# The mask's product moved from last to first in both attentions' score groups

## The chip, the cores and the metric

One core of one Trainium2 chip runs the whole kernel. The metric is device time in microseconds (us) of one execution; the kernel before takes 940.6 us (median of 3 runs, 940.55 to 940.61).

## The reference, cut to what matters

One layer of a streaming encoder on 512 tokens of width 1024. A parallel token mixer (forgetting attention with 8 heads of 64, and an mLSTM with 4 heads of 128) is followed by a cross-attention on 256 memory tokens and by a squared-ReLU MLP. What the change touches are the logits of the two mixers:

```python
# forgetting attention
logits = jnp.einsum('bhqd,bhkd->bhqk', qi, kf) + ci[..., :, None] - c[..., None, :]
logits = jnp.where(kpos[None, :] <= qpos[:, None], logits, -jnp.inf)
p = jax.nn.softmax(logits, axis=-1)
...
# mLSTM (chunkwise in the reference)
Dlog = bcum[..., :, None] - bcum[..., None, :] + ig[..., None, :]
Dlog = jnp.where(tri, Dlog, -jnp.inf)
...
Dw = jnp.exp(Dlog - m_t[..., None])
sqk = jnp.einsum('bhcld,bhcsd->bhcls', qc, kc) * Dw
```

The kernel computes the mLSTM as one causal attention over all 512 tokens, with the same decay and mask.

## The kernel before, in words

**Products.** Nearly all of TensorE's work is dense products of a weight with an activation, each operand split into a high and a low part of type fp32r; three products (high by high, high by low, low by high) are summed into one PSUM bank. A "half" (line 1504) is 4 slabs of 128 rows, so 12 products of 128 x 128 by 512 columns.

**Order.** `make_steps` writes out one list of steps by hand. Each engine walks through the same list and does its own part of every step; semaphores tie the engines together. The attention's steps are put before or after numbered halves, so that TensorE runs dense products while VectorE (DVE) and ScalarE (ACT) do the softmax work.

**Forgetting attention.** It has 16 tasks: 4 pairs of heads times 4 blocks of 128 queries. Block i looks at 128(i+1) keys. A task lies two halves behind the one before. `pair_scores` (from line 1587) fills bank 2 for the first head of the pair and bank 3 for the second: four products of 64 rows each (line 1602: three for the split scores and one for the decay; the two heads use rows 0 to 63 and 64 to 127), then the mask. The mask's product (line 1604) is bf16, `ident_b` by `hide_b`, 128 x 128 by 128 columns; it adds -1e30 above the diagonal of the last 128 keys. The last mask product raises `s_fscore`. DVE takes the row maximum (line 1367), ACT the exponential (990), DVE normalises (1375), TensorE transposes (1614, `pair_turn`), ACT copies to SBUF, TensorE multiplies with the values (1629, `pair_values`). On TensorE a block of steps is values of an older task, transposes of the task before, then the scores of the new task.

**mLSTM.** It has 16 tasks too (4 heads times 4 query blocks), one half apart. `scores` (from line 1634) writes the plain product of `ml_q` and `ml_k` (fp32, line 1646, two passes in the trace) to bank 5; bank 2 or 3 takes the decay (64 rows, line 1647) and then the mask (line 1648), which raises `s_score`. DVE takes the maximum (1389), then two small operations (1391, 1393), ACT the exponential (1004), DVE the product (1398), which raises `s_prob`. The scores of task t wait for `s_prob` of task t-1. After each head DVE also normalises the head's output (lines 1410 to 1428), and TensorE transposes it (1693).

**Weights.** ACT rounds each slab to `w_hi` (line 795), DVE forms `w_lo` (line 1093); these stand in the same lists as the attention's steps.

Of the kernel before, what the change touches and what calls it, by code (L numbers as in the profile page):

```python
# [13 lines left out]
P = 128  # L14
# [6 lines left out]
FOX_HEADS, FOX_HD = 8, 64  # L21
# [372 lines left out]
def trunk(nc, x, mem, norm_mix, norm_xattn, norm_mem, norm_mlp, w_in, b_fox_f, b_mlstm_i, b_mlstm_f,  # L394
# [6 lines left out]
    with ExitStack() as ctx:  # L401
        def sem(name):
            return ctx.enter_context(nc.semaphore(name))

        def sb(name, shape, dt=F32):
            return ctx.enter_context(nc.sbuf_tensor(name, shape, dt))
# [3 lines left out]
        ident_b = sb("ident_b", [P, P], BF16)  # L410
        hide_b = sb("hide_b", [P, P], BF16)
        rows = FOX_HEADS + ML_HEADS
        pick = sb("pick", [P, rows], F32R)
# [35 lines left out]
        def at(name, kb, shape, dt=F32):  # L449
            return nc.alloc_sbuf_tensor_at(name, shape, dt, offset=a0 + int(kb * KB))  # L450
# [3 lines left out]
        decay = at("decay", -53, [P, P * NT * (NT + 1) // 2], F32R)  # L454
# [55 lines left out]
        bank = [two[i // 2][:, i % 2, :] for i in range(8)]  # L510
# [39 lines left out]
        s_score, s_peak, s_exp, s_prob = sem("s_score"), sem("s_peak"), sem("s_exp"), sem("s_prob")  # L550
# [24 lines left out]
        def taken(eng, g):  # L575

            eng.wait_ge(s_taken[g % 2], g // 2 + 1)
# [9 lines left out]
        def task(t):  # L587

            h, i = t // NT, t % NT
            return h, i, P * (i + 1)  # L590
# [21 lines left out]
        def decay_at(i):  # L612
            return P * i * (i + 1) // 2
# [836 lines left out]
        def _(pe):  # L1450
# [136 lines left out]
            def pair_scores(t):  # L1587
                p, i = t // NT, t % NT
                keys, tok = P * (i + 1), slice(P * i, P * i + P)
                cols = slice(decay_at(i), decay_at(i) + keys)  # L1590
                if t == 0:
                    pe.wait_ge(s_dlow, len(DECAY_TILES) + 1)
                if i == 0:
                    taken(pe, GROUP0[UNIT["fox_k"]] + p)
                if t >= 1:
                    pe.wait_ge(s_fexp, 2 * t)
                for q in range(4):
                    for d in range(2):
                        r = slice(FOX_HD * d, FOX_HD * d + FOX_HD)
                        still = pick[r, 2 * p + d:2 * p + d + 1].to_broadcast([FOX_HD, P]) if q == 3 else (fq_hi, fq_hi, fq_lo)[q][r, p, tok]  # L1600
                        moving = decay[r, cols] if q == 3 else (fk_hi, fk_lo, fk_hi)[q][r, p, 0:keys]
                        pe.matmul(bank[2 + d][:, 0:keys], still, moving, start=(q == 0), stop=False)  # L1602
                for d in range(2):
                    ins = pe.matmul(bank[2 + d][:, P * i:keys], ident_b[:], hide_b[:], start=False, stop=True)
                ins.then_inc(s_fscore, 1)

            def pair_turn(t):
# [26 lines left out]
            def scores(t):  # L1634
                h, i, keys = task(t)
                s = bank[2 + t % 2]
                cols = slice(decay_at(i), decay_at(i) + keys)
                if t == 0:
                    pe.wait_ge(s_silu, KT)
                    pe.wait_ge(s_fpt, N_FOX)  # L1640
                    pe.wait_ge(s_fexp, 2 * N_FOX)
                else:
                    pe.wait_ge(s_prob, t)
                if t >= 2:
                    pe.wait_ge(s_exp, t - 1)
                pe.matmul(bank[5][:, 0:keys], ml_q[:, h, P * i:P * i + P], ml_k[:, h, 0:keys], start=True, stop=True)  # L1646
                pe.matmul(s[:, 0:keys], pick[0:64, FOX_HEADS + h:FOX_HEADS + h + 1].to_broadcast([64, P]), decay[0:64, cols], start=True, stop=False)  # L1647
                pe.matmul(s[:, P * i:keys], ident_b[:], hide_b[:], start=False, stop=True).then_inc(s_score, 1)

            def x_scores(t):  # L1650
                h, i = (t - X0) // NT, t % NT
# [70 lines left out]
            for step, n in steps:  # L1722
# [4 lines left out]
                elif step == "parameters":  # L1727
                    pe.wait_ge(s_param, 16 * 4)
                    pe.transpose(bank[6][:, 0:n_param], param_rows[:], ident[0:n_param, 0:n_param])\
                      .then_inc(s_pturned, 1)  # L1730
                elif step == "gates":
                    gates()
                elif step == "gate_turn":
                    pe.wait_ge(s_grows, 1)
                    for i in range(NT):
                        ins = pe.matmul(bank[7][:, 16 * i:16 * i + 16], gate_rows[:, P * i:P * i + P],
                                        pick_row[0:48, :], start=True, stop=True)
                    ins.then_inc(s_gturn, 1)
                elif step == "decay":
                    decays()  # L1740
                elif step == "pair_scores":
                    pair_scores(n)
                elif step == "pair_turn":
                    pair_turn(n)
                elif step == "pair_values":
                    pair_values(n)
                elif step == "scores":
                    x_scores(n) if n >= X0 else scores(n)
                elif step == "turn":
                    turn(n)  # L1750
                elif step == "values":
                    values(n)
                elif step == "ml_turn":
                    ml_turn(n)
                elif step == "x_values":
                    x_values(n)
# [30 lines left out]
```

## Time and profile before

| | |
|---|---|
| median of 3 runs | 940.6 us |
| the profiled execution's own time | 940.86 us |
| its span | 939.1 us |
| TensorE (PE) busy | 926.9 us, 99% |
| weight loads (PEld) busy | 757.5 us, 81% |
| VectorE busy | 552.2 us, 59% |
| ScalarE busy | 427.8 us, 46% |
| granted TensorE clock | 0.998 of full speed |

Busy times are of one profiled execution. PE is the matmul part of TensorE and PEld its weight loads, which can lie beside the matmuls. A matmul's end is modelled, so its start and the distance to the next start are better read than its duration. The forgetting attention's scores lie between 86 and 205 us, the mLSTM's between 224 and 297 us.

### The profile page before, as it was taken

How to read it: one execution, taken by the hardware profiler on the slowest of the kernel's cores; microseconds unless marked ns; L12 is line 12 of the kernel's file. 1: busy time of each engine (PE TensorE's matmuls, PEld its weight loads, DVE VectorE, ACT ScalarE, POOL GpSimd, SP SyncE). 2: the span in 40 equal slices, each digit the busy share in tenths (PEclk: the TensorE clock that was granted, in tenths of full speed). 3: DMA queues.
4: the chain of work that ended last, by engine and by line, in shares of the span. 5: the costliest groups of instructions: out<-in, count | busy, mean ns of one | idle time of the engine just before them, and what ended most of it. 6: DMA issues, size and time to landing. Idle time of an engine off the chain costs nothing.

```text
span 939.1 us, 11910 instructions
## 1 busy us (share of the span) xinstructions
PE 926.9 (99%) x4614; PEld 757.5 (81%) x4614; DVE 552.2 (59%) x997; ACT 427.8 (46%) x744; POOL 15.6 (2%) x40
## 2 busy tenths in 40 slices
PE   7999999999999999999999999999999999999997
PEld 6878777777777888889888778988888888888886
DVE  5534777423557654777234544668847966885543
ACT  5544466534424323335344543466346436634523
POOL 5000000000000000000000000000000000000000
PEclk9999999999999999999999999999999999999999
DMA  7411222022201462343521432120631261062202
GB/s 273 134 36 56 89 91 77 28 76 90 90 1 45 132 227 89 112 135 112 180 90 45 135 135 90 45 90 1 206 108 45 90 224 45 1 223 92 89 1 90
DMA packets 44687, 92.10 MB, mean 98 GB/s; under 512 B 1764, under 2 KB 1864, under 8 KB 44632
## 3 DMA queue, kind: packets, MB, share of 16 engines
q1 hardware_dynamic: 43048, 86.02, 27.0%
q0 software_dynamic: 1568, 5.32, 1.7%
q8 instruction: 37, 0.61, 0.3%
q14 instruction: 18, 0.15, 0.1%
q10 hardware_dynamic: 16, 0.00, 0.0%
HBM read 89.24 MB, written 2.10 MB: 97 GB/s over the span
## 4 chain that ended last, share of the span: by engine, by line
PE 95%; DVE 2%; ACT 2%; issue 0%; POOL 0%; ACTq 0%; DVEq 0%; POOLq 0%
PE bank L1504 70%; PE bank L1535 12%; PE bank L1659 1%; PE bank L1708 1%; PE bank L1602 1%; PE bank L1629 1%; PE bank L1614 1%; PE bank L1548 1%; PE bank L1646 1%; PE bank L1686 1%; PE bank L1673 1%; ACT w_hi L795 1%; PE bank L1647 0%; PE bank L1720 0%; DVE w_lo L1093 0%
## 5 line engine op out<-in xcount | busy, mean ns | idle before, releaser
L1504 PE MATMUL bank<-act_hi,w_hi 128*128 128x512 f32 (+1 forms) x640 | 247.7, 387 | 0.1
L1504 PE MATMUL bank<-act_hi,w_lo 128*128 128x512 f32 (+1 forms) x640 | 242.7, 379 | 0.0
L1504 PE MATMUL bank<-act_lo,w_hi 128*128 128x512 f32 (+1 forms) x640 | 242.4, 379 | 0.0
L1089 DVE TENSOR_TENSOR w_lo<-stage,w_hi 128x1024 fp32r<-128x1024 f32 x130 | 153.2, 1222 | 65.0 <-ACT w_hi L795 64.7
L795 ACT ACTIVATE w_hi<-stage 128x1024 fp32r<-128x1024 f32 x130 | 130.3, 1051 | 90.4 <-PE bank L1504 31.7
L1504 PEld LDWEIGHTS bank<-act_hi,w_lo 128*128 128x128 f32 x640 | 120.4, 188 | 23.1
L1504 PEld LDWEIGHTS bank<-act_hi,w_hi 128*128 128x128 f32 x640 | 120.6, 188 | 21.9 <-DVE w_lo L1089 0.6
L1504 PEld LDWEIGHTS bank<-act_lo,w_hi 128*128 128x128 f32 x640 | 120.6, 188 | 21.4
L1504 PE MATMUL bank<-w_hi,act_hi 128*128 128x512 f32 (+1 forms) x264 | 102.9, 390 | 3.8 <-DVE act_lo L1321 2.0
L1504 PE MATMUL bank<-w_hi,act_lo 128*128 128x512 f32 (+1 forms) x264 | 101.2, 383 | 0.0
L1504 PE MATMUL bank<-w_lo,act_hi 128*128 128x512 f32 (+1 forms) x264 | 101.1, 383 | 0.0
L1093 DVE SCALAR_TENSOR_TENSOR w_lo<-stage,gain_col,w_hi 128x512 fp32r<-128x512 f32 x88 | 60.3, 747 | 26.4 <-ACT w_hi L795 26.4
L1504 PEld LDWEIGHTS bank<-w_hi,act_hi 128*128 128x128 f32 x264 | 49.6, 188 | 14.5 <-issue 2.8
L1504 PEld LDWEIGHTS bank<-w_hi,act_lo 128*128 128x128 f32 x264 | 49.6, 188 | 9.8
L795 ACT ACTIVATE w_hi<-stage,gain_col 128x512 fp32r<-128x512 f32 x88 | 56.2, 713 | 2.5 <-PE bank L1504 2.5
L1504 PEld LDWEIGHTS bank<-w_lo,act_hi 128*128 128x128 f32 x264 | 49.7, 188 | 9.3 <-issue 0.2
L1221 DVE TENSOR_TENSOR act_lo<-ff,act_hi 128x512 fp32r<-128x512 f32 (+1 forms) x32 | 18.9, 592 | 60.2 <-ACT act_hi L795 60.0
L865 ACT ACTIVATE ff<-bank 128x512 f32<-128x512 f32 x32 | 19.0, 594 | 49.1 <-PE bank L1504 49.1
L1535 PE MATMUL bank<-w_hi,act_hi 128*128 128x512 f32 x96 | 37.3, 389 | 0.0
L1535 PE MATMUL bank<-w_lo,act_hi 128*128 128x512 f32 x96 | 37.3, 389 | 0.0
L1535 PE MATMUL bank<-w_hi,ff_lo 128*128 128x512 f32 x96 | 37.3, 389 | 0.0
L795 ACT ACTIVATE act_hi<-bank 128x512 fp32r<-128x512 f32 x32 | 17.6, 596 | 35.1 <-PE bank L1548 29.7
(290 smaller groups left out, 1290.7 us busy)
## 6 DMA issues: line engine op xcount, KB each, us to landing
stage<-in_w_in SPq DMA_DIRECT2D x20, 1024.0 KB, 4.9
stage<-in_w_mlp_in SPq DMA_DIRECT2D x16, 1024.0 KB, 5.2
stage<-in_w_mlp_out SPq DMA_DIRECT2D x16, 1024.0 KB, 5.5
stage<-in_w_xkv SPq DMA_DIRECT2D x8, 1024.0 KB, 5.0
stage<-in_w_mix_out SPq DMA_DIRECT2D x4, 1024.0 KB, 4.9
stage<-in_w_xq SPq DMA_DIRECT2D x4, 1024.0 KB, 6.0
stage<-in_w_xo SPq DMA_DIRECT2D x4, 1024.0 KB, 5.0
x_tok<-in_x SPq DMA_DIRECT2D x4, 512.0 KB, 7.0
```

What stands on the lines that cost most here:

```text
L795: return act.activation(dst, src, ACT.Copy, **k)
L865: act.activation(ff[:, t, :], b[:], ACT.Relu).then_inc(free, 1)
L1089: dve.tensor_tensor(w_lo[:, r:r + 2, :], stage_pair(pair), w_hi[:, r:r + 2, :].bitcast(F32), ALU.subtract).then_inc(s_low, 1)
L1093: ins = dve.scalar_tensor_tensor(w_lo[:, r + d, :], stage_pair(pair)[:, d, :], gain_of(pair, d), w_hi[:, r + d, :].bitcast(F32), ALU.mult, ...
L1221: dve.tensor_tensor(act2_lo[:, t, toks], ff[:, t, toks], act2_hi[:, t, toks].bitcast(F32), ALU.subtract).then_inc(s_al, 1)
L1504: ins = pe.matmul(dst, still[q], moving[q], start=(k == 0 and q == 0), stop=(k == nk - 1 and q == 2))
L1535: ins = pe.matmul(dst, s, w[:, slab % RING, :], start=(u == 0 and g == 0), stop=(u == 3 and g == 2))
L1548: ins = pe.transpose(bank[2 + 2 * (n % 2) + b][:, P * q:P * q + P], scaled[:, n % 2, P * k:P * k + P], ident[:])
L1602: pe.matmul(bank[2 + d][:, 0:keys], still, moving, start=(q == 0), stop=False)
L1614: ins = pe.transpose(bank[4 + d][:, P * j:P * j + P], (prob, prob_b)[t % 2][:, d, P * j:P * j + P], ident[:])
L1629: ins = pe.matmul(bank[6 + p % 2][r:r + FOX_HD, P * i:P * i + P], fox_v[:, j, col:col + FOX_HD], prob_t[:, d, P * j:P * j + P], start=(j = ...
L1646: pe.matmul(bank[5][:, 0:keys], ml_q[:, h, P * i:P * i + P], ml_k[:, h, 0:keys], start=True, stop=True)
```

## The change

The mask's product becomes the first into its bank and starts the sum. The scores and decays are added to it; the last decay product raises the semaphore. The number and shapes of the products are the same. In the mLSTM the mask also goes ahead of the product into bank 5.

```diff
@@ pair_scores
+                for d in range(2):
+                    pe.matmul(bank[2 + d][:, P * i:keys], ident_b[:], hide_b[:], start=True, stop=True)
                 for q in range(4):
                     for d in range(2):
...
-                        pe.matmul(bank[2 + d][:, 0:keys], still, moving, start=(q == 0), stop=False)
-                for d in range(2):
-                    ins = pe.matmul(bank[2 + d][:, P * i:keys], ident_b[:], hide_b[:], start=False, stop=True)
+                        ins = pe.matmul(bank[2 + d][:, 0:keys], still, moving, start=False, stop=(q == 3),
+                                        skip_group_check=True)
                 ins.then_inc(s_fscore, 1)
@@ scores
+                pe.matmul(s[:, P * i:keys], ident_b[:], hide_b[:], start=True, stop=True)
                 pe.matmul(bank[5][:, 0:keys], ml_q[:, h, P * i:P * i + P], ml_k[:, h, 0:keys], start=True, stop=True)
-                pe.matmul(s[:, 0:keys], pick[0:64, FOX_HEADS + h:FOX_HEADS + h + 1].to_broadcast([64, P]), decay[0:64, cols], start=True, stop=False)
-                pe.matmul(s[:, P * i:keys], ident_b[:], hide_b[:], start=False, stop=True).then_inc(s_score, 1)
+                pe.matmul(s[:, 0:keys], pick[0:64, FOX_HEADS + h:FOX_HEADS + h + 1].to_broadcast([64, P]), decay[0:64, cols],
+                          start=False, stop=True, skip_group_check=True).then_inc(s_score, 1)
```

## Rows read from the trace of the kernel before

**Rows 1.** The page: busy time by engine, and the chain that ended last.
```profile
PE 926.9 (99%) x4614; PEld 757.5 (81%) x4614; DVE 552.2 (59%) x997; ACT 427.8 (46%) x744; POOL 15.6 (2%) x40
PE 95%; DVE 2%; ACT 2%; issue 0%; POOL 0%; ACTq 0%; DVEq 0%; POOLq 0%
```

**Rows 2.** Chain of waits, 200 to 300 us: start us, us, what.
```profile
275.30 0.18 PE bank L1648
...
275.50 0.70 DVE ml_m L1389
...
283.76 2.74 DVE w_lo L1093 x4
...
294.06 0.56 DVE prob L1398
...
294.68 1.12 PE bank L1646 x2
```

**Rows 3.** Timeline round a forgetting-attention task: start us, us, engine, line, tiles, count.
```profile
85.97 0.39 PE L1504 MATMUL bank<-act_lo,w_hi 128*128 128x512 f32 x1
85.98 0.19 PEld L1504 LDWEIGHTS bank<-act_hi,w_lo 128*128 128x128 f32 x1
86.20 0.39 PE L1504 MATMUL bank<-act_hi,w_lo 128*128 128x512 f32 x1
86.52 0.19 PEld L1602 LDWEIGHTS bank<-fk_hi,fq_hi 64*128 64x128 f32 x2 [0.35 <-issue]
...
86.91 0.27 PE L1602 MATMUL bank<-decay,pick 64*128 64x128 f32 x2
87.11 0.11 PEld L1604 LDWEIGHTS bank<-hide_b,ident_b 128*128 128x128 bf16 x2
87.11 0.28 PE L1604 MATMUL bank<-hide_b,ident_b 128*128 128x128 bf16 x2
87.18 0.19 PEld L1504 LDWEIGHTS bank<-act_hi,w_hi 128*128 128x128 f32 x1
...
87.52 0.39 PE L1504 MATMUL bank<-act_lo,w_hi 128*128 128x512 f32 x1
```

**Rows 4.** Line 1604: duration ns min/median/max, first and last start us, forms.
```profile
L1604 PE MATMUL bank<-hide_b,ident_b x32: 219/224/230, 87.1 to 203.7; 128*128 128x128 bf16 x32
```

**Rows 5.** Timeline: the first two dense products behind a product of 60 rows.
```profile
43.52 0.50 PE L1504 MATMUL bank<-act_hi,w_hi 128*128 128x512 f32 x1
...
43.85 0.39 PE L1504 MATMUL bank<-act_lo,w_hi 128*128 128x512 f32 x1
```

**Rows 6.** Timeline round an mLSTM task of 512 keys.
```profile
236.40 1.02 PE L1646 MATMUL bank<-ml_k,ml_q 128*128 128x512 f32 x2
237.35 0.50 PE L1647 MATMUL bank<-decay,pick 64*128 64x512 f32 x1
237.78 0.23 PE L1648 MATMUL bank<-hide_b,ident_b 128*128 128x128 bf16 x1
...
238.05 0.69 DVE L1389 TENSOR_REDUCE ml_m<-bank 128x1 f32<-128x512 f32 x1 [2.25 <-PE bank L1648]
238.13 0.40 PE L1504 MATMUL bank<-act_lo,w_hi 128*128 128x512 f32 x1
```

**Rows 7.** Timeline round two mLSTM tasks of 384 keys, tasks 2 and 6.
```profile
232.09 0.91 PE L1646 MATMUL bank<-ml_k,ml_q 128*128 128x384 f32 x2
...
232.93 0.44 PE L1647 MATMUL bank<-decay,pick 64*128 64x384 f32 x1
...
250.02 0.81 PE L1646 MATMUL bank<-ml_k,ml_q 128*128 128x384 f32 x2
250.76 0.43 PE L1647 MATMUL bank<-decay,pick 64*128 64x384 f32 x1
```

**Rows 8.** Who waited for whom, 218 to 306 us: us in total, times, longest us.
```profile
PEld bank L1646 <- DVE ml_den L1398: 1.5, 2, 1.2
PE bank L1646 <- DVE ml_den L1398: 1.0, 1, 1.0
```

## The prediction

> **What bounds the kernel now.** First the page: TensorE's matmuls are busy 99% of the span and 95% of the chain that ended last runs on PE [rows 1]. So a nanosecond that the change adds to TensorE's stream is a nanosecond of the result, unless TensorE waits for something there anyway. Second the chain of waits: through the forgetting attention it never leaves PE. In the mLSTM it leaves PE once: behind the mask at 275.30, which ends the scores of task 11, it goes to DVE at 275.50 and stays on DVE and ACT, with weight splits and the head's normalisation between the softmax steps, until PE resumes at 294.68 [rows 2]. That stretch of 19.2 us is not set by PE, so what PE loses inside it (tasks 12 to 14) is covered, up to the 1.0 us that PE idles at its end [rows 8]; what PE loses before 275.3 is paid. Third the timeline, read by the distance between starts: what does each change of shape on TensorE cost, since the change moves these.
>
> **What a change of shape costs, read from before.** Dense products start 0.23 apart (85.97, 86.20), and the weights of the next are loaded beside the running one (load at 85.98) [rows 3]. The first 64-row product starts 0.32 behind the last dense one, and its load starts only then: 0.09 more than 0.23, a drain. From 64 rows back to 128 it drains again: last decay pair at 86.91, mask load at 87.11, 0.20 for some 0.11 of work. A load that could not be hidden costs about 0.10 if its type is fp32: tasks 2 and 6 have the same shape, but task 2 had to wait, and from `ml_q`'s first product to the decay it takes 0.84 (232.09 to 232.93) against 0.74 (250.02 to 250.76) [rows 7]. The same shows in the dense product behind 60 rows: 0.33 to the next start, where 0.23 is usual [rows 5]. For the bf16 `ident_b` the load reads 0.11 for two, an exposed cost of some 0.03 [rows 3].
>
> **Forgetting attention, 16 tasks.** Removed at the end: from the last decay pair (86.91) to the second dense product (87.52) is 0.61 [rows 3]. In it are a drain, the exposed bf16 load, two mask products and the fp32 load of the first dense product, half covered by the second mask (load at 87.18). After the change the decay pair is followed by a dense product: 0.20 with the drain, as now to the mask, then 0.33 with a bare load [rows 5]. That is 0.53 to 0.54, 0.07 less. Added in front: two masks. The first starts where the 64-row product now would without a drain. Its pair takes 0.28 in the row where one takes 0.22 [rows 3, 4], so the second starts 0.06 behind; then 0.05 of work (128 columns, by the dense product's 0.21 for 512) and the drain of 0.10 to the 64 rows. The front grows from 0.32 (drain included) to 0.23 + 0.06 + 0.15 = 0.44, by 0.12; behind the transposes the same difference, 0.11 to 0.12. The four 64-row pairs between don't change. Sum per task: +0.12 - 0.07 = +0.045, and for 16 tasks +0.7 us. The change saves no drain (two before, two after); it trades a cheap exposed bf16 load for the dearer fp32 load that half of a mask had covered.
>
> **mLSTM, 16 tasks.** Now `ml_q`'s load hides behind the transposes, and the decay's and mask's loads are exposed. After it the mask's load hides, but the mask runs 0.05 and `ml_q`'s fp32 load, which can only start with it, takes 0.107: from the mask's start to `ml_q`'s 0.107. Behind the decay, from the mask at 237.78 to the second dense product at 238.13 is 0.35 now [rows 6]; it becomes 0.33 to 0.34 [rows 5]. Sum +0.107 - 0.015 = +0.09 for a task that waits for nothing. Which tasks pay it:
> tasks 3 to 10: 8 x 0.09 = +0.74. Task 0: +0.01, since `ml_q`'s load is bare today too, behind the values' narrower products. Tasks 1 and 2: +0.02 together. Task 2 waits for `s_prob` [rows 7, 8], its load is bare already, and its release does not come later with task 1's scores: in front of task 1's maximum DVE has an operation that hangs on an earlier dense half. Task 11 up to its signal: the mask now ends at 275.46, which releases DVE at 275.50 [rows 2]; by task 3's rows the signal comes 0.43 + 0.23 = 0.66 behind the decay's start. Then it is the decay's own end, 0.50 [rows 6]. With the +0.107 ahead of it that is -0.05. Tasks 12 to 14: 0, inside DVE's stretch. Task 15: 0.00, bare load before and after. Sum +0.72.
>
> No transfer and no DVE or ACT instruction is added or moved. Nothing new waits: the mask takes over the waits (`s_fexp`, `s_prob`, `s_exp`) that stood before the first score product, with the same products queued behind it.
>
> **The total.** +0.7 + 0.72 = +1.4 us. The profiled execution's own time is 940.86, so 942.3 for one like it; it stands 0.26 above the median of 940.6, and against that the forecast is 942.0. Bounds of the unseen pieces. A bf16 load behind an fp32 product of the same 128 rows is in no row. Fully hidden it costs 0, as each dense load does [rows 3]; at the other end it waits for a drain and is bare, 0.09 + 0.03 = 0.12 for each of the 16 + 9 tasks on the path, +3.0. I take 0: the nearest rows are the loads of the same row count, all hidden. The mask followed by a 64-row product is not seen either: with the drain as after dense products and transposes, or, at the other end, without it, -0.10 x 16 = -1.5. I take the drain, for it stands at both changes of row count seen. The second mask's start may lie 0.05 to 0.07 behind the first's: 16 x 0.01 = 0.2 either way.
>
> The Trainium skill ("TensorE: Matmul & The Clock Gate", The mechanism) says that weight loads overlap running matmuls "only when row_grp differs". By that the mask's load behind a full-row product would be bare, which leads to the dearer end. The trace disagrees: the dense load at 85.98 runs beside the product of 85.97, both of 128 rows [rows 3]; and where the row count does change, at 86.52, the load waited.
>
> **Rivals.**
> (B) *The mask's bf16 weights are not prefetched behind fp32 products*, by type or by the wait that now stands on that load. It decides in front of every task: +3.0, so 945.0. For it: no row shows the pair; against it: `ml_q`'s load carries the same kind of wait and hides. Half of it (bare but no drain) gives 25 x 0.03 = +0.75, 942.8.
> (C) *No drain between the mask and the 64-row products*: 942.0 - 1.5 = 940.5; if their load hides as well, 16 x 0.05 less, 939.7. Against it: every full-row product before a 64-row one drains.
> (D) *The earlier signal is worth more.* `s_score` comes 0.16 sooner after the decay. If DVE's stretch of 19.2 us did hang on PE at one or two more points, or if tasks 3 to 10 waited too, each would give back 0.16. All eight together give -1.3, so 940.7. Against it: only three waits on `s_prob` are there, before tasks 2, 14 and 15 [rows 8].
>
> **How the numbers follow.** Forecast 942.0, chance 0.60, own range 941.4 to 942.6. B whole 0.10 (945.0), B in part 0.12 (942.8), C 0.10 (940.5, or 939.7), D 0.08 (940.7). A measurement of this kernel can tell about 0.2% from no change, 1.9 us: above 942.5 is slower, below 938.7 faster. Slower: B whole, most of B in part, and the forecast's upper edge, 0.22. Faster 0.04. Within 0.2%: 0.74. The range that holds 8 in 10 leaves out B whole and C's far end: 940.2 to 943.2.
>
> **What would show it.** In the profile after: `ident_b`'s load starting while the transposes or dense products still run (else B); mask to first 64-row start 0.20 to 0.22 for the pair (0.11 if C); the last decay pair to the second dense product 0.53 where it was 0.61; in the mLSTM mask to second `ml_q` product longer by 0.10; DVE's maximum starting 0.50 to 0.54 behind the decay at 512 keys; one stretch on DVE of 19.2 us, with PE's idle at its end shrunk from 1.0 to about 0.7. The forecast is wrong if TensorE's stretch from 86 to 210 us doesn't grow by 0.6 to 0.8, or if the mLSTM's chain leaves PE at another place.

## The result, and the profile after

The changed kernel takes 941.99 us (median of 22 runs, 941.78 to 942.57) against 940.7 us (22 runs, 940.46 to 941.1) beside it: ratio 1.0014, 95% interval 1.0008 to 1.002, so +1.3 us. The forecast was 942.0.

The profiled execution took 942.57 us, its span is 940.8. From its page, the busy line and the chain by engine:

```profile
span 940.8 us, 11910 instructions
...
PE 927.9 (99%) x4614; PEld 758.3 (81%) x4614; DVE 552.1 (59%) x997; ACT 428.0 (45%) x744; POOL 15.5 (2%) x40
...
PE 94%; DVE 2%; ACT 2%; DMA 1%; issue 0%; SPq 0%; ACTq 0%; DVEq 0%
```

PE and PEld are busy 1.0 and 0.8 us longer, the others within 0.2. The DMA share is new and has nothing to do with the change: in this execution the first weights landed later (the first half-size slabs of `in_w_in` 7.4 us after their issue, before 6.0), and the last dense product ahead of the first task starts at 86.67 instead of 86.20 (+0.47). In the twelve traces of this document that start lies anywhere from 85.88 to 86.83. The two profiled executions are 1.71 apart, less 0.47 is 1.24; the medians say 1.29.

The timeline round the same forgetting-attention task as in [rows 3] (columns: start us, us, engine, line, tiles, count):

```profile
86.67 0.39 PE L1504 MATMUL bank<-act_hi,w_lo 128*128 128x512 f32 x1
86.89 0.12 PEld L1598 LDWEIGHTS bank<-hide_b,ident_b 128*128 128x128 bf16 x2 [0.26 <-issue]
86.90 0.29 PE L1598 MATMUL bank<-hide_b,ident_b 128*128 128x128 bf16 x2
87.11 0.19 PEld L1604 LDWEIGHTS bank<-fk_hi,fq_hi 64*128 64x128 f32 x2
...
87.50 0.27 PE L1604 MATMUL bank<-decay,pick 64*128 64x128 f32 x2
87.70 0.19 PEld L1504 LDWEIGHTS bank<-act_hi,w_hi 128*128 128x128 f32 x1
...
88.04 0.39 PE L1504 MATMUL bank<-act_lo,w_hi 128*128 128x512 f32 x1
```

Front: 86.67 to 87.11 is 0.44, where it was 0.32. Tail: 87.50 to 88.04 is 0.54, where it was 0.61. The load at 87.70 starts together with its product; before, at 87.18, it ran under the second mask.

The timeline of the mLSTM task in [rows 6]:

```profile
237.40 0.10 PEld L1647 LDWEIGHTS bank<-hide_b,ident_b 128*128 128x128 bf16 x1
...
237.51 0.22 PE L1647 MATMUL bank<-hide_b,ident_b 128*128 128x128 bf16 x1
237.51 0.30 PEld L1648 LDWEIGHTS bank<-ml_k,ml_q 128*128 128x128 f32 x2
237.56 1.08 PE L1648 MATMUL bank<-ml_k,ml_q 128*128 128x512 f32 x2
...
238.57 0.49 PE L1649 MATMUL bank<-decay,pick 64*128 64x512 f32 x1
...
238.99 0.50 PE L1504 MATMUL bank<-act_hi,w_hi 128*128 128x512 f32 x1
...
239.10 0.69 DVE L1389 TENSOR_REDUCE ml_m<-bank 128x1 f32<-128x512 f32 x1 [2.36 <-PE bank L1649]
239.32 0.39 PE L1504 MATMUL bank<-act_lo,w_hi 128*128 128x512 f32 x1
```

The mask's own load (237.40) is hidden, `ml_q`'s starts only with the mask (237.51): from there to the decay it is 1.06, where `ml_q`'s product to the decay took 0.95. DVE starts 0.53 behind the decay, where it was 0.70.

The chain of waits over the stretch of [rows 2]:

```profile
276.89 0.44 PE bank L1649
...
277.36 0.70 DVE ml_m L1389
...
285.61 2.74 DVE w_lo L1093 x4
...
295.91 0.56 DVE prob L1398
...
296.53 0.23 PE bank L1647
```

It leaves PE at the same place and comes back 19.17 us later; before it was 19.18. PE's idle at its end, against [rows 8]:

```profile
PEld bank L1647 <- DVE ml_den L1398: 1.3, 2, 1.1
...
PE bank L1647 <- DVE ml_den L1398: 0.9, 1, 0.9
```

Where the 1.24 us lie, from the starts of the two timelines:

- The 16 forgetting tasks, each from the product ahead of it to the second one behind it, sum to 23.13 us before and 23.79 after: +0.66. The dense products between them take 0.04 less.
- The mLSTM up to DVE's start on task 11: +0.77 (275.50 to 277.36 is +1.86, less 0.47 for the later start and 0.62 for the forgetting attention).
- DVE's stretch: 0.00. Behind it: -0.12, by one wait that is 0.15 shorter, shown next.

These add up to 1.27, against 1.24 by the two executions' times.

The place behind the stretch is the first product of head 3 with the values (line 1686, in the changed kernel 1688). The kernel makes it wait for `s_mgate`, which DVE's line 1433 raises when it has read head 1's bank; in DVE's list that line stands right behind task 15's softmax. The timeline before (window 298.9:299.8), then after (300.6:301.5):

```profile
298.93 0.68 DVE L1433 SCALAR_TENSOR_TENSOR ml_h<-ml_th,bank 128x512 f32<-128x512 f32 x1
...
299.19 0.39 PE L1504 MATMUL bank<-act_hi,w_lo 128*128 128x512 f32 x1
...
299.71 0.35 PE L1686 MATMUL bank<-ml_v,prob_t 128*128 128x128 f32 x1
```

```profile
300.65 0.68 DVE L1433 SCALAR_TENSOR_TENSOR ml_h<-ml_th,bank 128x512 f32<-128x512 f32 x1
...
301.07 0.39 PE L1504 MATMUL bank<-act_hi,w_lo 128*128 128x512 f32 x1
...
301.44 0.35 PE L1688 MATMUL bank<-ml_v,prob_t 128*128 128x128 f32 x1
```

From the last dense product to the values it is 0.52 before and 0.37 after, where two dense products are 0.23 apart; in both, the values start 0.10 us behind the end of line 1433. The profile names no releaser for this wait; the kernel's semaphore and the equal 0.10 do. DVE began task 15's maximum 1.75 us behind the start of that task's scores before and 1.61 after, so line 1433 ends sooner too. Head 2's first values wait in the same way behind task 11's softmax: 0.53 behind the last dense product (278.80), after the change 0.37.

### The profile page after: what moved, and what is told of

Read it like the earlier page. It is cut to its first block, busy times and chain, and to the rows that moved or that the text cites. A ratio compares the mean times of both kernels' runs of the same rounds, so it can differ in the third digit from the quotient of the medians.

```text
span 940.8 us, 11910 instructions
## 1 busy us (share of the span) xinstructions
PE 927.9 (99%) x4614; PEld 758.3 (81%) x4614; DVE 552.1 (59%) x997; ACT 428.0 (45%) x744; POOL 15.5 (2%) x40
## 4 chain that ended last, share of the span: by engine, by line
PE 94%; DVE 2%; ACT 2%; DMA 1%; issue 0%; SPq 0%; ACTq 0%; DVEq 0%
PE bank L1504 71%; PE bank L1535 12%; PE bank L1661 1%; PE bank L1710 1%; PE bank L1604 1%; PE bank L1630 1%; PE bank L1615 1%; PE bank L1548 1%; DMA stage<-in_w_in 1%; PE bank L1648 1%; PE bank L1688 1%; PE bank L1675 1%; ACT w_hi L795 1%; PE bank L1649 0%; DVE w_lo L1093 0%
```

## The experiments

Each ran against the kernel before on the same chip; what a diff does not name is the kernel before. The 95% intervals of these ratios are some 0.8 us wide to either side or more, so where two forecasts lie closer than that, the distances in the traces decide between them. Where a place in a trace is compared, it is counted from the last dense product ahead of the first forgetting task.

**Half of the change each.** `fox_only` has the diff of `pair_scores`, `ml_only` that of `scores`.

> Only the forgetting attention has its mask first; the mLSTM is as before. Theory (T), TensorE's stream alone: each of the 16 tasks grows by 0.04 us, front +0.11, tail -0.07, and nothing later gives it back, so +0.6 to +0.7 us against the kernel before. Rival (W), the time of the whole change comes from the mLSTM and what hangs on it: +0.0 to +0.2 here.

Measured: 941.54 against 940.68, ratio 1.0008 (0.9999 to 1.0016), +0.9 us. In its trace the 16 tasks sum to 23.79 us, as in the full change, and DVE starts on task 11 at 276.23, counted from that dense product 0.64 later than before. The rival W gave at most 0.2; by the trace it is out.

> Only the mLSTM has its mask first. T: tasks 3 to 10 grow by 0.087 us each (0.70), tasks 0 to 2 by 0.03 together, task 11's signal comes 0.05 sooner, tasks 12 to 14 are covered by VectorE's stretch: +0.6 to +0.7 us, and PE's idle ahead of task 15 falls from 1.2 by some 0.1. Rival (U), all 16 tasks pay: 16 x 0.087 = +1.4. The two halves of the change should add up to its +1.3.

Measured: 941.61 against 940.68, ratio 1.0008 (1.0000 to 1.0017), +0.9 us. In its trace DVE starts on task 11 51.85 us behind the product ahead of task 0, before 51.08: +0.77. Tasks 0 to 2 grow by 0.01 and task 11 up to DVE's start by -0.05, so it is not all tasks that pay, and U (1.4) is out by the trace; the time alone, with its interval up to 1.6, would not exclude it. The two halves add up to 1.8 where the whole is 1.3, inside the intervals; by the traces the shares up to task 11 are 0.64 and 0.77. Head 3's first values stand 0.36 behind the last dense product in this trace, as in the full change, and 0.53 in that of `fox_only`.

**The mask between plain product and decay.**

```diff
                 pe.matmul(bank[5][:, 0:keys], ml_q[...], ml_k[...], start=True, stop=True)
+                pe.matmul(s[:, P * i:keys], ident_b[:], hide_b[:], start=True, stop=True)
-                pe.matmul(s[:, 0:keys], pick[...], decay[0:64, cols], start=True, stop=False)
-                pe.matmul(s[:, P * i:keys], ident_b[:], hide_b[:], start=False, stop=True).then_inc(s_score, 1)
+                pe.matmul(s[:, 0:keys], pick[...], decay[0:64, cols], start=False, stop=True,
+                          skip_group_check=True).then_inc(s_score, 1)
```

> Only the mLSTM is changed, and its mask stands between the plain product and the decay: it still starts the sum in its bank, but ml_q's fp32 weights are again loaded behind the transposes. T: a task of 3 to 10 grows by 0.035 to 0.04 us (mask's work 0.056, plus the dense product's bare load, minus the mask's own bare load and its half cover), not by 0.087; task 11's signal comes 0.11 sooner: +0.15 to +0.25 us in all. Rival (P), the price is that of a mask that starts the sum in place of one that ends it, wherever it stands in front of the decay: +0.6 to +0.7 as with the mask ahead of both.

Measured: 940.93 against 940.68, ratio 1.0002 (0.9993 to 1.0011), +0.25 us. Its timeline at 512 keys:

```profile
236.57 0.30 PEld L1646 LDWEIGHTS bank<-ml_k,ml_q 128*128 128x128 f32 x2
...
236.67 1.02 PE L1646 MATMUL bank<-ml_k,ml_q 128*128 128x512 f32 x2
237.11 0.10 PEld L1647 LDWEIGHTS bank<-hide_b,ident_b 128*128 128x128 bf16 x1 [0.24 <-issue]
...
237.53 0.22 PE L1647 MATMUL bank<-hide_b,ident_b 128*128 128x128 bf16 x1
237.68 0.18 PEld L1648 LDWEIGHTS bank<-decay,pick 64*128 64x128 f32 x1 [0.48 <-issue]
```

`ml_q`'s load is ahead of its product again, the mask's runs 0.4 ahead. A task of 3 to 10 is 0.027 to 0.039 us longer than before (0.27 in sum), in the change it was 0.080 to 0.093 (0.69). So the price is set by which load stands behind the mask, not by the mask's starting the sum; P (0.6 to 0.7) is out by the tasks' lengths, though the time's interval would still hold it. Two things T had not counted are in the trace: tasks 0 and 1 grow by 0.04 each, and the dense products between the tasks by 0.10 in sum; 0.06 is given back behind task 15's start.

**The mask first, and once more at the end.**

```diff
@@ pair_scores of fox_only, behind the loop over q
+                ins = pe.matmul(bank[3][:, P * i:keys], ident_b[:], hide_b[:], start=False, stop=True,
+                                skip_group_check=True)
```

> The forgetting attention with the mask first for both heads, and for the second head of each pair the same mask added once more at the end (its hidden entries become -2e30, the output stays the same). So 16 more products than with the mask first alone. T: behind the 64-row pair this bf16 product takes over the drain and covers half of the dense product's fp32 load, so it costs 0.015 us a task: +0.24 on top of the forgetting attention's own +0.65, +0.9 us in all; from the last decay pair to the second dense product 0.55 against 0.54. Rival (P), a product costs its work and its bare load wherever it stands (0.056 + 0.03): +1.4 on top, +2.0 us in all.

Measured: 941.79, ratio 1.0010 (1.0001 to 1.0019), +1.1 us, 0.25 above `fox_only`. The tail of task 4 in its timeline:

```profile
116.71 0.27 PE L1604 MATMUL bank<-decay,pick 64*128 64x128 f32 x2
...
116.92 0.23 PE L1606 MATMUL bank<-hide_b,ident_b 128*128 128x128 bf16 x1
116.92 0.20 PEld L1504 LDWEIGHTS bank<-act_hi,w_hi 128*128 128x128 f32 x1
...
117.27 0.40 PE L1504 MATMUL bank<-act_lo,w_hi 128*128 128x512 f32 x1
```

From the decay pair to the second dense product 0.56, with one product more in it. The 16 tasks sum to 24.10 us, 0.31 more than in `fox_only`: 0.019 a task, where the second mask of a pair starts 0.056 behind the first. With the dense products between the tasks it is 0.24. T held, P (+1.4) fell: the place behind a drain, in front of an fp32 load, is nearly free, and this is the place from which the change took the mask.

**The order turned, and the signal with it.** In `ml_last` decay and mask stand ahead of the plain product, whose end raises `s_score`; in `ml_early` the mask raises `s_score`; in `ml_early_free` decay and mask also don't wait for `s_prob`.

```diff
@@ scores of ml_early_free (ml_early: the wait on s_prob stays at the top)
                 pe.matmul(s[:, 0:keys], pick[...], decay[0:64, cols], start=True, stop=False)
                 pe.matmul(s[:, P * i:keys], ident_b[:], hide_b[:], start=False, stop=True).then_inc(s_score, 1)
+                if t > 0:
+                    pe.wait_ge(s_prob, t)
+                pe.matmul(bank[5][:, 0:keys], ml_q[...], ml_k[...], start=True, stop=True).then_inc(s_plain, 1)
@@ vector, ahead of line 1398
+                    dve.wait_ge(s_plain, n + 1)
```

For `ml_early`:

> Both attentions have the mask last again. In the mLSTM the decay and the mask go ahead of the plain product, and the mask's end raises s_score; the plain product has a semaphore of its own, which VectorE waits for only before line 1398. TensorE's stream per task is as long as before (202 + 430 + 39 + 518 + 431 + 227 = 1847 ns at 512 keys against 1848). T: task 11's maximum starts 0.86 us sooner, VectorE's stretch of 19.2 us moves with it, and PE's idle of 1.17 at its end pays it back: -0.8 to -0.9 us against before. Rival (H), the stretch hangs on TensorE at a later point too, by a weight slot that ScalarE waits for or by a transpose: it gets longer by up to 0.86, and the time is that of before.

For `ml_early_free`:

> As the one before, and the decay and mask of a task no longer wait for s_prob, only the plain product does. T: in front of task 15 the decay and the mask (0.63 us) run in PE's idle; of the 1.17 + 0.19 us of idle in the mLSTM some 0.1 is left: -1.1 to -1.3 us against before. Rival (H): as the one before.

For `ml_last`:

> The mLSTM's decay and mask go ahead of the plain product, but s_score is raised only by the plain product's end; all else as in ml_early. It parts that run's gain (-1.83 us measured) into the order on TensorE and the earlier signal. T: the order alone gives 0.19 in task 0 and 0.15 in task 15, whose loads are bare in the kernel before, and 0.1 in task 2; task 11's signal comes 0.06 later than before: -0.3 to -0.4 us. Rival (O), the order is what paid: -1.2 or more.

Measured: `ml_last` 940.12 against 940.75, ratio 0.9993 (0.9984 to 1.0002), -0.6 us; `ml_early` 938.93 against 940.76, 0.9981 (0.9972 to 0.9990), -1.8 us; `ml_early_free` 938.27, 0.9974 (0.9964 to 0.9984), -2.5 us. The earlier signal pays 1.2 of `ml_early`'s gain. O asked for 1.2 or more from the order, which the interval of `ml_last` would still hold; its trace gives 0.52 (0.38 up to DVE's start on task 11, 0.14 in task 15 and behind), so O is out. H is out too, for DVE's stretch keeps its length (19.17). In the timeline of `ml_early`, task 11:

```profile
273.56 0.50 PE L1648 MATMUL bank<-decay,pick 64*128 64x512 f32 x1
...
273.99 0.23 PE L1649 MATMUL bank<-hide_b,ident_b 128*128 128x128 bf16 x1
...
274.05 1.08 PE L1650 MATMUL bank<-ml_k,ml_q 128*128 128x512 f32 x2
274.25 0.69 DVE L1390 TENSOR_REDUCE ml_m<-bank 128x1 f32<-128x512 f32 x1 [2.88 <-PE bank L1649]
```

DVE starts at 274.25 instead of 275.50, and PE resumes at task 15 at 293.43 instead of 294.68, both 1.25 sooner by the clock and 1.30 counted from the first task: 0.86 by the signal, 0.19 and 0.20 by tasks 0 and 2, whose loads stood bare, and 0.03 between the tasks. A further 0.14 is gained in task 15, and 0.38 at head 3's first values, which wait for DVE behind that task's softmax: a second place at which the early signal pays. All three forecasts fell short: `ml_early` gained 1.8 where 0.8 to 0.9 was put, since only the signal at task 11 was counted; `ml_early_free` 2.5 where 1.1 to 1.3 was put; `ml_last` 0.6 where 0.3 to 0.4 was put.

**The decay on all 128 rows.** Rows 64 to 127 of the mLSTM's columns of `pick` are made zero, so the product is the same.

```diff
-                pe.matmul(s[:, 0:keys], pick[0:64, ...].to_broadcast([64, P]), decay[0:64, cols], ...)
+                pe.matmul(s[:, 0:keys], pick[:, ...].to_broadcast([P, P]), decay[:, cols], ...)
@@ gpsimd: the ones of rows 64 and 96 only in the forgetting heads' columns
+                c = 16 if r < 64 else FOX_HEADS
+                fill(pool.affine_select(out=pick_row[:, 0:c], in_=pick_row[:, 0:c], ..., pattern=[[-1, c]], ...))
```

With the mask last (`ml_rows`):

> Mask last everywhere. The mLSTM's decay product takes all 128 rows instead of 64 (in rows 64 to 127 its stationary column is zero), so no product of the mLSTM changes the row count. T: both drains and all bare loads but half of one go: a task of 512 keys takes 109 + 432 + 427 + 227 + 110 + 227 = 1.53 us where it took 1.85, one of 128 keys 0.77 where it took 1.03. Tasks 0, 3 to 10 and task 11's signal give 10 x 0.26 to 0.31, task 15 0.3 and task 2 up to 0.3; unless a softmax in between is late (task 7's release is 0.5 us ahead of it now): -2.2 to -3.2 us against before. Rival (L), only the bare loads go, the drains belong to the change of the stationary operand itself: half of it, -1.2 to -1.5. Rival (R), rows have no part in it: 0.

With the mask first (`ml_rows_first`):

> The mLSTM with the decay on all 128 rows, and with its mask first as in the change; the forgetting attention as before. T: without a change of row count all loads but one half hide in either order, so a task takes as long as with the mask last on 128 rows (within 0.01 us), and the change's cost of 0.087 us per mLSTM task is gone: within 0.1 us of the run with the mask last. Rival (P), the mask in front costs 0.087 us a task whatever stands behind it: 0.7 us more than that run.

Measured: 937.66 with the mask last, ratio 0.9966 (0.9954 to 0.9978), -3.1 us; 937.30 with the mask first, 0.9963 (0.9951 to 0.9975), -3.5 us. A task of 512 keys went from 1.85 to 1.55 us, one of 128 from 1.03 to 0.75: both drains and the bare loads were the price of the change of row count. T's range was 2.2 to 3.2; L and R are out. The timeline, mask last:

```profile
236.60 0.19 PEld L1648 LDWEIGHTS bank<-decay,pick 128*128 128x128 f32 x1 [0.24 <-issue]
236.63 0.79 PE L1648 MATMUL bank<-decay,pick 128*128 128x512 f32 x1
...
237.26 0.10 PEld L1649 LDWEIGHTS bank<-hide_b,ident_b 128*128 128x128 bf16 x1 [0.47 <-issue]
237.26 0.23 PE L1649 MATMUL bank<-hide_b,ident_b 128*128 128x128 bf16 x1
...
237.61 0.39 PE L1505 MATMUL bank<-act_lo,w_hi 128*128 128x512 f32 x1
```

The decay's start is recorded early here, 0.03 behind `ml_q`'s second product, and its 0.79 holds the rest of that product; the distance from `ml_q`'s second product (236.60) to the mask, 0.66, is what can be read.

On 128 rows the mask first costs nothing in sum: that run is 0.4 us below the one with it last, where P asked for 0.7 above. T had asked for 0.1 either way; of the 0.4, a shorter stall at tasks 2 and 7 (1.66 for 1.76, 1.70 for 1.76) is 0.17, the rest lies within the runs' spread. A task is not as long in either order to 0.01, as T had it: of those that wait for nothing, one of 128 keys takes 0.04 longer with the mask first, one of 256 or more 0.02 less, and tasks 3 to 6 and 8 to 10 are equal in sum (to 0.01).

**Both together.** `ml_rows_early` is `ml_early_free` with the decay on 128 rows.

> The decay on 128 rows together with decay and mask ahead of the plain product, s_score raised by the mask, and only the plain product waiting for s_prob. On 128 rows alone PE idled 5.0 us in the mLSTM for s_prob. T: with scores up to 1.2 us earlier most of that goes: -5 to -6 us against before. Rival (V), VectorE's stretches of some 19 us are a bound of their own once TensorE is ahead of them: the idle stays above 2.5 us and the gain is -3.5 to -4.5.

Measured: 935.36 against 940.75, ratio 0.9943 (0.9930 to 0.9957), -5.4 us, and 6.6 under the changed kernel. Who waits for `s_prob` in the mLSTM, first `ml_rows`, then `ml_rows_early` (us in total, times, longest):

```profile
PEld bank L1647 <- DVE ml_den L1399: 3.0, 4, 1.5
...
PE bank L1647 <- DVE ml_den L1399: 2.0, 3, 1.3
```

```profile
PEld bank L1651 <- DVE ml_den L1401: 1.3, 1, 1.3
PE bank L1651 <- DVE ml_den L1401: 1.2, 1, 1.2
```

One wait is left, at task 15. The two rows count the same time on TensorE's two parts (PE's idle and its loads'); my expectation had added them up to 5.0, where PE idled 2.0. T's 5 to 6 us came true in spite of it. V asked for more than 2.5 of idle and is out; what is left of it is DVE's stretch ahead of task 15, which still makes PE wait.

## Why the prediction was right

- **TensorE's stream is the bound.** Shown: the cost lies in the distances between TensorE's starts, and DVE's, ACT's and the transfers' work is unchanged. Only up to task 11 does all of it count; behind that DVE's stretch covers it, as forecast.
- **Forgetting attention, +0.7.** Measured +0.66 in the tasks (0.028 to 0.055 each), +0.62 with the dense products between them; front +0.11 to +0.12 and tail -0.07 as worked out. Shown by `fox_only`, and for the tail the reason (a bf16 load and half a cover given up for a bare fp32 load) by `fox_twice`. One size in it was off: a bare bf16 load costs 0.01 and not 0.03 (the mask's successor starts 0.066 behind it where its load was bare, 0.056 where it was hidden). The 0.05 of work for a mask was taken from 0.21 for 512 columns; no row shows 0.21, dense products start 0.224 to 0.236 apart, and with the load hidden the next start is 0.056 behind a mask.
- **mLSTM, +0.72.** Measured +0.77 up to DVE's start on task 11. The +0.09 of tasks 3 to 10 came out as 0.080 to 0.093, 0.69 in sum where 0.74 was put; tasks 0 to 2 0.01; task 11 up to DVE's start -0.05, as said. Left is +0.13 that no step of mine had: in six of the stretches between two tasks the dense products keep 0.02 more distance each. In both kernels the first ten or so of them behind a group start 0.224 to 0.236 apart and the later ones 0.226 to 0.227, and the order of the group changes how these distances fall; why, no run here tells. That `ml_q`'s load is the price of the tasks is shown by `ml_between`.
- **Task 15, 0.00.** Measured -0.12 from its scores to the end, by a wait 0.15 shorter, not in the task but at head 3's first values behind it. This is a term that the prediction put at nothing: the earlier signal lets DVE end task 15's softmax, and then line 1433, sooner, and TensorE waits there.
- **DVE's stretch.** Length 19.17 as before, and PE's idle at its end fell from 1.0 to 0.9, not to 0.7 as I wrote: head 2's first values (278.80) had waited in the same way and wait 0.16 less now, which took up the first part. No effect on the time.
- **Rivals.** B whole did not come. B in part did in three places (tasks 0 and 1 of the forgetting attention, task 1 of the mLSTM), at 0.01 each and not 0.03. C did not: the drain between mask and 64 rows is there, 0.15 from the second mask's start in all 16 tasks. D, an earlier signal that gives back some 0.16 at one more point, came true once on the path, at head 3's first values (0.15); [rows 8] lists only waits on `s_prob`, and this one is on `s_mgate`.
- **Sum.** +1.4 forecast, +1.3 measured. The priced terms came out right one by one to within 0.07 us. That the sum did so well is in part luck: the two pieces that the prediction did not have, +0.13 in the mLSTM's dense products and -0.12 behind task 15, cancel.

## What to carry to other kernels

When TensorE is the bound, ask of a reordering which weight load stands behind which product: the load has to fit under the product ahead, so put the cheap load (bf16) behind a drain and a short product in front of a load that would be bare anyway. A change of row count costs a drain of about 0.1 us and a bare load, twice; filling the rows up with zeros was worth 3 us here, more than any order of the products. And raise the signal for the softmax from the product that it needs, not from the last of the group. When you look for what an earlier signal can pay, list every wait of TensorE on the engine that does the softmax, also those for another operation that stands behind it in that engine's list.

## What the runs showed of the hardware that was not expected

The types are the kernel's; the trace writes f32 for fp32 and fp32r alike. The bf16 load of `ident_b` is pulled ahead behind fp32 products (load at 237.40, product at 237.51, behind transposes; 0.4 ahead in `ml_between`), but not behind fp32r products of the same 128 rows: at 86.89 it starts 0.22 behind the dense product of 86.67, and at 237.26 in `ml_rows` behind the decay, each time together with its own product. There is no drain with it, and it costs about 0.01 us. The dense fp32r loads are hidden behind fp32r products [rows 3]. Why the pair of bf16 behind fp32r is different no run here tells.

A change of the column count drains as one of the row count does. In the trace before, the forgetting attention's products with the values load 64 columns: the first starts 0.318 behind the dense product ahead of it in all 16 tasks (a 64-row product starts 0.319 behind it), and the first product of 128 columns behind them 0.203 behind the last (a 64-row product starts 0.202 behind the transposes). No run changed that count.
